# A hybrid decoder layer on one core: the first two F tiles by Strassen's products, interleaved

## The reference

```python
n = rmsnorm(h, ln1_g);  proj = n @ w_in                       # 1024 -> 1536 columns
y_pool = pool_mixer(...);  y_lru = rg_lru(...) * gelu(u_gate) # the two mixers, 512 wide each
mix = concat(rmsnorm(y_pool), rmsnorm(y_lru));  h = h + mix @ w_out
n2 = rmsnorm(h, ln2_g)
h = h + (silu(n2 @ w_ffn_gate) * (n2 @ w_ffn_up)) @ w_ffn_down   # D_FF = 2816 = 22 tiles of 128
return rmsnorm(h, lnf_g)
```

## Time and profile before

| | us |
|---|---|
| median of 3 runs (lowest, highest) | 896.62 (896.47, 896.67) |
| the profiled execution | 896.3 |
| its span, first to last instruction | 894.5 |
| PE busy | 882.7 (99%) |
| PEld busy | 725.7 (81%) |
| DVE busy | 613.7 (69%) |
| ACT busy | 396.1 (44%) |
| POOL busy | 273.6 (31%) |

### The profile page before, as it was taken

How to read it: one execution, slowest core, us unless ns; L and a number is a source line. 1 busy time by engine, 2 the same in 40 slices (tenths; PEclk the granted TensorE clock), 3 DMA queues, 4 the chain that set the end, 5 groups by cost and what they waited for, 6 DMA issues and landing times.

```text
span 894.5 us, 11037 instructions
## 1 busy us (share of the span) xinstructions
PE 882.7 (99%) x3980; PEld 725.7 (81%) x3980; DVE 613.7 (69%) x848; ACT 396.1 (44%) x654; POOL 273.6 (31%) x209
## 2 busy tenths in 40 slices
PE   7999999999999999999999999999999999999997
PEld 6877788888888888888888888888888888888886
DVE  5778996655679856556565664656638975787667
ACT  6689733533565323332233332333234444454456
POOL 0000032733345655545554555555540000000000
PEclk9999999999999999999999999999999999999999
DMA  9033011132020423223232332413239933333324
GB/s 322 9 96 93 24 48 48 47 118 71 1 72 0 150 75 130 83 95 136 88 130 74 102 130 69 156 56 121 95 107 377 398 104 96 95 96 99 101 83 188
DMA packets 94318, 98.01 MB, mean 110 GB/s; under 512 B 5764, under 2 KB 63672, under 8 KB 94264
## 3 DMA queue, kind: packets, MB, share of 16 engines
q1 hardware_dynamic: 83736, 78.16, 26.1%
q10 hardware_dynamic: 10528, 19.15, 7.1%
HBM read 70.81 MB, written 24.38 MB: 106 GB/s over the span
## 4 chain that ended last, share of the span: by engine, by line
PE 98%; DVE 1%; DMA 0%; ACT 0%; issue 0%; DVEq 0%; ACTq 0%
PE bank L2112 23%; PE bank L2113 23%; PE bank L2114 23%; PE bank L2000 5%; PE bank L2002 5%; PE bank L2001 5%; PE bank L1944 3%; PE bank L1945 3%; PE bank L1946 3%; PE bank L2021 1%; PE bank L1978 1%; PE bank L1957 1%; DMA h<-in_x 0%; PE bank L1966 0%; DVE nT_lo L1308 0%
## 5 line engine op out<-in xcount | busy, mean ns | idle before, releaser
L723 POOL TENSOR_TENSOR r_lo<-gu_raw,r_hi 128x512 fp32r<-128x512 f32 x84 | 115.7, 1378 | 83.4 <-ACT r_hi L1023 83.3
L723 POOL TENSOR_TENSOR r_lo<-wsum_S,r_hi 128x512 fp32r<-128x512 f32 x63 | 98.1, 1558 | 109.6 <-ACT r_hi L1023 109.6
L2112 PE MATMUL bank<-T_hi,r_lo 128*128 128x512 f32 x336 | 130.8, 389 | 0.0
L2114 PE MATMUL bank<-T_hi,r_hi 128*128 128x512 f32 x336 | 130.7, 389 | 0.0
L2113 PE MATMUL bank<-T_lo,r_hi 128*128 128x512 f32 x336 | 130.7, 389 | 0.0
L2113 PE MATMUL bank<-d_lo,h_hi 128*128 128x512 f32 (+1 forms) x312 | 120.5, 386 | 0.0
L2114 PE MATMUL bank<-d_hi,h_hi 128*128 128x512 f32 (+1 forms) x312 | 120.5, 386 | 0.0
L2112 PE MATMUL bank<-d_hi,h_lo 128*128 128x512 f32 (+1 forms) x312 | 120.5, 386 | 0.0
L1023 ACT CAST r_hi<-gu_raw 128x512 fp32r<-128x512 f32 x84 | 52.2, 621 | 143.6 <-PE bank L2114 143.6
L2112 PE MATMUL bank<-nT_hi,r_lo 128*128 128x512 f32 x252 | 98.0, 389 | 0.0
L2113 PE MATMUL bank<-nT_lo,r_hi 128*128 128x512 f32 x252 | 98.0, 389 | 0.0
(11 more groups left out here) (247 smaller groups left out, 1637.5 us busy)
## 6 DMA issues: line engine op xcount, KB each, us to landing
h_raw<-hid_ops ACTq DMA_DIRECT2D x72, 256.0 KB, 2.6
gu_raw<-in_w_ffn_gate SPq DMA_DIRECT2D x22, 512.0 KB, 3.7
gu_raw<-in_w_ffn_up SPq DMA_DIRECT2D x22, 512.0 KB, 4.8
hid_ops<-hid SPq DMA_DIRECT2D x44, 256.0 KB, 2.3
dn<-in_w_ffn_down SPq DMA_DIRECT2D x44, 256.0 KB, 9.8
hid_ops<-hsum_S SPq DMA_DIRECT2D x33, 256.0 KB, 2.6
w_raw<-in_w_in SPq DMA_DIRECT2D x11, 512.0 KB, 4.5
h<-in_x SPq DMA_DIRECT2D x8, 512.0 KB, 6.6
```

The lines of the kernel that those rows point to most:

```text
L723: pool.tensor_tensor(lo_of(n)[:], a_block(f, name), f32(hi_of(n)[:]), ALU.subtract)\
L2112: pe.matmul(bank, s_lo, m_hi, start=(opens and j == 0), stop=False, skip_group_check=True)
L2114: ins = pe.matmul(bank, s_hi, m_hi, start=False, stop=(closes and j == n - 1), skip_group_check=True)
```

## The change

- **F tiles 0 and 1 both by Strassen's products, interleaved.** The order is M1, M2, M3, M6, M7, M5, M4 and each product is done for f = 0 and then for f = 1. 15 products become 14. M3 gets a PSUM bank of its own in these two tiles, and `gate_second` adds two banks there. The last two token tiles are turned after the first and after the second product. Entries are numbered anew: the first four are A11 and A12 of both tiles, entries 4 and 5 S4, 6 and 7 S2, 8 and 9 S3, 10 and 11 S1, 12 and 13 A22.
- **Preparation.** The weight sums of F tiles 0 and 1 are made during the token tiles m = 3 to 6 of stage 2. T1's sum is apart (`t1_sum`), its first part ahead of the last variance of stage 2. `nT_hi` and `nT_lo` of B12 aren't made any more (B12 enters only through the T sums); GpSimd makes the low parts of B22 (`nT_lo_c`), VectorE those of B21 (`nT_lo_b`).
- **Operations.** VectorE's sums of two SBUF tensors there (weight sums, T sums, low parts of T and of B21, the last step of the reciprocal root) are scalar_tensor_tensor with a scalar of 1.0 instead of tensor_tensor.
- **Loads.** F tile 1's up weights no longer wait for the end of stage 2; F tile 2's weights wait for entry 12, F tile 3's for entry 13.
- **The beginning of stage 1.** In `project` the high times high and low weights come first, the low activations last; for (c, i) = (1, 0) all passes with the weights' low part come at the end. ScalarE takes the last squares of the first four tiles after two of the second half's casts.
- `sq_scr` and the low part of the last w_out piece move to other places; the latter is written in three instructions instead of two.

```diff
-        SECOND = ("M1", "M2", "M6", "M7", "M5", "M4", "M3")
+        FIRST = ("M1", "M2", "M3", "M6", "M7", "M5", "M4")
         def entry(f, pr):
-            return 4 + 7 * (f - 1) + products(f).index(pr)
+            return 2 * FIRST.index(pr) + f if f < 2 else 7 * f + PRODUCTS.index(pr)
...
         def chain_bank(f, c):
-            return psum[(4 if f == 1 else 3 * (f % 2)) + c]
+            return psum[(4, 2, 6)[c] + f] if f < 2 else psum[3 * (f % 2) + c]
...
             for f in range(2, FT):
-                sp_q.wait_ge(r_lo_ok, 4 if f == 2 else entry(f - 2, "M3") + 1)
+                sp_q.wait_ge(r_lo_ok, entry(f - 2, "M4" if f < 4 else "M3") + 1)
                 load_gu(f)
...
+            def combine(out_, a, b, op):
+                return dve.scalar_tensor_tensor(out=out_, in0=a, scalar=1.0, in1=b, op0=ALU.mult, op1=op)
...
+            def t1_sum(g):
+                s1, s2 = t_part(g, 0), t_part(g, 1)
+                dve.wait_ge(raw_ok, 2 * (5 + 2 * g) + 1)
+                dve.wait_ge(nlo_a_ok, 2 * g + 2)
+                combine(raw[0][:, :, s1], raw[0][:, :, s2], raw[0][:, :, s1], ALU.subtract).then_inc(t_ok, 1)
+
             def t_sums(g):
                 s1, s2 = t_part(g, 0), t_part(g, 1)
...
                 dve.wait_ge(t_ok, 3 * g + 1)
-                dve.tensor_tensor(raw[0][:, :, s2], raw[1][:, :, s2], raw[0][:, :, s2], ALU.subtract).then_inc(t_ok, 1)
-                dve.tensor_tensor(raw[1][:, :, s2], raw[1][:, :, s2], raw[0][:, :, s1], ALU.subtract).then_inc(t_ok, 1)
+                dve.wait_ge(raw_ok, 2 * (5 + 2 * g) + 2)
+                combine(raw[0][:, :, s2], raw[1][:, :, s2], raw[0][:, :, s2], ALU.subtract).then_inc(t_ok, 1)
+                dve.wait_ge(nlo_c_ok, 2 * g + 2)
+                combine(raw[1][:, :, s2], raw[1][:, :, s2], raw[0][:, :, s1], ALU.subtract).then_inc(t_ok, 1)
...
+            t1_sum(1)
             t_sums(1)
-            hidden1(0)
             t4_sums()
-            weight_sums(1, ("S1",))
-            for name, g in T_HI[0:4]:
+            for name, g in T_HI[0:5]:
                 t_lo(name, g)
-            hidden2(0)
-            for name, g in T_HI[4:6]:
+            second_sum(0)
+            t_lo("T1", 1)
+            second_sum(1)
+            for name, g in T_HI[6:]:
                 t_lo(name, g)
+            third_sum(0)
+            third_sum(1)
+            up_second(0)
+            gate_second(0)
+            weight_sums(2, ("S1",))
+            up_second(1)
+            gate_second(1)
+            hidden2(0)
+            up_first(0)
+            hidden1(0)
+            weight_sums(2, ("S4",))
+            up_first(1)
+            hidden1(1)
+            hidden2(1)
...
+                if (c, i) == (1, 0):
+                    pe.wait_ge(w_hi_ok, w_count(1))
...
+                if late:
+                    pe.wait_ge(w_lo_ok, w_count(1))
+                    for k in range(KT):
+                        ins = pe.matmul(bank, lo_[:, k], nT_hi[:, k, half(0)], start=False, stop=(k == KT - 1))
...
+            gate_up_product(0, "M1")
+            transposes(2 * TT - 2, xs2)
+            gate_up_product(1, "M1")
+            transposes(2 * TT - 1, xs2)
+            for pr in FIRST[1:]:
+                for f in range(2):
+                    gate_up_product(f, pr)
```

More of the change, by code:

```diff
@@ L357, in wo_low @@
         def wo_low(q, k):
-            return wo_lo3[k // 2][:, k % 2] if q == 3 else wo_lo[q % 2][:, k]
+            if q == 3:
+                return wo_lo3[:, k] if k < 2 else wo_lo3_end[k - 2][:]
+            return wo_lo[q % 2][:, k]
         t2 = t2b[:]
@@ L1065, in silu1 @@
                 p = f // 2
[L1066 to L1071, removed]
+                act.wait_ge(ent_ok, done(entry(f, "M2")))
+                if f == 1:
+                    act.wait_ge(r_lo_ok, entry(1, "M3") + 1)
                 if p > 0 and f % 2 == 0:
@@ L1157, in split_dn @@
                 act.copy(d_hi[s % STEPS][:], dn[D_BLOCK[pr], k][:]).then_inc(d_hi_ok, 1)
-            for f in range(1, FT):
-                for pr in products(f):
+            for f in range(2, FT):
+                for pr in PRODUCTS:
                     n = entry(f, pr)
-                    if pr == "M1" and f >= 2:
+                    if pr == "M1":
                         copy_m1(f)
@@ L1280, in rsqrt @@
                 if ready is None:
-                    step(dve.tensor_tensor(out_, out_, tmp_, ALU.mult))
+                    step(combine(out_, out_, tmp_, ALU.mult))
                 else:
@@ L1637, in t_lo @@
                 dve.wait_ge(t_hi_ok, T_HI.index((name, g)) + 1)
-                dve.tensor_tensor(T_lo[b][:, :, c], raw[b][:, :, c], f32(tile[:, :, t_part(g, j)]), ALU.subtract)\
+                combine(T_lo[b][:, :, c], raw[b][:, :, c], f32(tile[:, :, t_part(g, j)]), ALU.subtract)\
                     .then_inc(t_lo_ok, 1)
@@ L1766, in _ @@
+            up_first(0)
[4 more added lines that the diff above has]
+            hidden2(1)
+            for f in range(2, FT):
+                second_sum(f)
+                if f == 2:
+                    hidden_sums(0)
+                if f + 1 < FT:
+                    weight_sums(f + 1, ("S1",))
+                third_sum(f)
+                up_second(f)
                 if f + 1 < FT:
@@ L1993, in project @@
                 _, hi_, lo_ = w_tiles(c)
+                bank = pj[u % 4][:]
+                late = (c, i) == (1, 0)
                 for n, k in enumerate(X_ORDER[i]):
```

408 lines of the change are left out of this document (206 added, 202 removed).

## The result

The kernel after takes **900.47 us** (median of six, 898.96 to 900.82) against 896.64 for the kernel before (896.44 to 896.91): ratio 1.004, 95% interval 1.0028 to 1.0052. It is slower by 3.8 us where 2.2 were forecast, and the 900.8 at the upper end of the stated range just holds it. The profiled execution has a span of 899.0, 4.5 more than before, and is the longest of its six.

A forecast was written before the change was run, and what follows sets the result against it. PE, busy 882.7 of 894.5 us, was taken as the bound. Terms -2.7 - 0.5 + 3.4 + 0.3 + 1.2 + 0.5 = +2.2 gave 898.8 us (chance 0.38; own range 897.6 to 900.2, stated range 892.8 to 900.8).

The forecast's parts named there:

- Rival 1: VectorE and GpSimd overlap ahead of M6 of F tile 0, so no wait there: 893.4 us, chance 0.30.
- rival 3: F tile 2's weights land 1 to 2 us later than 295.3 and delay its first product: 900.2 us, chance 0.10.
- The product: F tile 0 takes seven products instead of eight, saving PE 12 matmuls, 2.72 us.
- Stage 1: PE's gaps near 14 and 17 us close at the beginning of stage 1: 0.5 us saved, bounds 0.2 and 0.6.
- rival 4: The product is saved but stage 1's 0.5 us isn't, as the DMA feeds it; inside all ranges, no separate chance.
- M6: F tile 0's seventh product waits 3.4 us for T sums, as VectorE and GpSimd exclude each other; bounds 2.9 and 4.0.
- u3: The hidden sums of F tiles 0 and 1 follow in one heap and put off u3: 0.5 us.
- After it, 0.3: Following M6, M7 of F tile 0 waits for u2, behind the low part of T1: 0.3 us (0 to 2).
- the upper bound there: If GpSimd waits for several VectorE instructions in a row, entry 7 is late by 3 x 1.2, costing another 2 us.
- Costs that something hides: Stage 2's added weight sums, 2.0 us in token tiles 3 and 5, are covered by VectorE's idle 1.8; 0.2 left over.
- u2 of F tile 2: Entry 12 delays F tile 2's load, VectorE stands before its weight sums, PE waits for u2: 1.2 us.
- Rival 2: VectorE catches up: M6 waits 3.4 us and nothing else does, 896.8 us, no change; chance 0.22.

The follow-up runs named there:

- engine: The kernel after, with four of GpSimd's subtractions ahead of M6 made by VectorE instead: 898.90 us, ratio to before 1.0025.
- twice: The kernel after, with GpSimd making each of four subtractions ahead of M6 twice, with the same result: 905.27 us, ratio to before 1.0095.
- tt: The kernel after, with its sums by tensor_tensor instead of scalar_tensor_tensor with a factor of 1: 899.92 us, ratio to before 1.0037.
- stage1: The kernel before, with only the change's part in stage 1: 896.06 us against 896.59, ratio 0.9995.
- Early: The kernel after, with F tiles 0 and 1's weight sums in token tiles 0 to 2 of stage 2 instead of 3 to 6: 899.05 us, ratio to before 1.0025.
- Order: The kernel after, with VectorE's first weight sum of F tile 2 moved behind three sums that need no load: 899.55 us, ratio to before 1.0032.
- combo2: combo, with F tile 2's first weight sum one place earlier and its u3 ahead of F tile 3's weight sums: 894.93 us, ratio to before 0.998.
- combo: The kernel after with the edits of engine, Order and Early at once: 896.81 us, ratio to before 1.0003.

## Why the prediction was right or wrong

**Where it held.** The direction, and the mechanism that makes it: VectorE and GpSimd take turns. Moving GpSimd's four instructions away (engine) and doubling them (twice) moved the stalls up to M6 by -1.7 and +5.0 with VectorE's list growing in the one and unchanged in the other. Rival 1, which wanted side by side, is refuted by both. The form of the sums changes nothing (tt). The size is another matter: 900.47 lies above the forecast's own range (897.6 to 900.2), and the figure nearest to it is that of rival 3, whose mechanism no trace shows.

**The terms.** The product: 2.72, as forecast. Stage 1: 0.5 forecast, 0.5 by the median of stage1, 0.6 by the traces; rival 4 fell. M6: 3.4 forecast, 2.94 measured. From the end of the last `normalise` to M6 I had 15.4; it took 14.86 (262.21 to 277.07), and the 0.54 between them are the nine 0.06 added for the longer form, which isn't longer: two such sums take 2.36 at 272.30, a step of 1.14 as before. The 1.28 that I had taken it from is that of `normalise`, which multiplies by a column and a row. u3: 0.5 and 0.47. "After it, 0.3" stood for u2 of F tile 0; the stall came at the next product instead, 0.52, and from entry 7. Its cause is ScalarE's queue, which the prediction lists: GpSimd stood 7.04 for the cast and then needed 2.12 (278.23), one turn; it did not wait for several of VectorE's, as the upper bound there had it.

**The step that failed** is "Costs that something hides". I set the weight sums of stage 2 against VectorE's idle 1.8 us in a token tile and found 0.2 left over. But the sums fall where GpSimd splits the first four entries. The same exclusion that I used for M6 makes one of the three sums 1.77 instead of 0.68, and it does so again in later token tiles. Nor does the running ahead of PE cover it: what is late is not a bank but `normalise`. The last one ended at 262.21, where I had 261.0, so PE waited 0.96 for xs where I had written "no stall". Early took the sums out of these token tiles; that `normalise` ended at 260.64, and the stall was gone. That the meetings with GpSimd decide, and not the sums' own length, is an estimate from rows: the two that take 1.77 and 1.78 add 2.2 us, more than the 1.2 by which `normalise` is late.

**The term mis-sized** is u2 of F tile 2: 1.2 forecast, 1.96 measured. The chain was the one I named (entry 12, the load, VectorE before its weight sums). VectorE got its load at 295.84 instead of 295.3, and behind it four of its instructions, not three, met one of GpSimd at 1.73 to 1.78 each, and a fifth took 1.00. Order shows that the wait hung in the main on the standing before the load: with other work there, u2 comes 2.5 earlier, 0.8 of it by an earlier load. Rival 3 (the load holds up the first product) had no stall in any trace of the kernel after. Rival 2 would have had M6 alone.

0.96 + 0.76 + 0.2 (entry 7) + 0.4 (small steps) - 0.46 (M6) - 0.1 (stage 1) = 1.8: from 2.2 to 3.95.

## What to carry to other kernels

If two engines take turns at a resource, apply it to every stretch in which both have work, the ones written down as "hidden" too; a helper's instruction then costs its time twice, once on its own engine and once on the other. An in-order list should wait for a load only behind all that needs no load. And a saved product is worth its matmuls only if everything that it wants earlier can be had earlier: here, with five places in the lists put right, 1.0 of the 2.72 us is left in combo2's trace (1.6 less, 0.6 of it from stage 1); the rest went into two waits and small steps.

## What the runs showed of the hardware

- **TensorE can fall to half its clock behind a stall.** In tt, behind the wait of 2.80, PE's timeline steps by 0.43 instead of 0.23, from 277.63 to 279.76:

```profile
277.07 0.77 PE L2184 MATMUL bank<-T_hi,r_lo 128*128 128x512 f32 x1 [2.80 <-DVE T_lo L1294]
277.63 0.63 PE L2185 MATMUL bank<-T_lo,r_hi 128*128 128x512 f32 x1
278.06 0.63 PE L2186 MATMUL bank<-T_hi,r_hi 128*128 128x512 f32 x1
```

  By stretches (us, then busy time of PE, PEld, DVE, ACT and POOL, granted clock, DMA) twice has 0.52 behind its stall of 4.8, near the lower level of 1.2 GHz, and full clock 6 us later:

```profile
282.00:288.00 6.00, 5.97 (x15) 4.69 (x16) 5.92 (x4) 0.41 (x1) 3.24 (x2) 0.52 0.00 0
288.00:294.00 6.00, 6.00 (x28) 4.96 (x27) 3.92 (x5) 3.35 (x5) 3.57 (x3) 1.00 0.00 0
```

  It came behind waits of 1.9, 2.4, 2.8, 2.8 and 4.8 us, and did not behind waits of 1.8, 2.1, 2.8 and 2.8 in the two traces of the kernel after, nor behind any of 1.3 or less. (The expectation of twice counts engine, whose half pace stands behind 1.9, among the waits of 2.4 or more.) Other runs of one kernel seem to differ in it too: of the six of the kernel after three have a mean granted clock of 0.996 or 0.997, where the profiled runs with half pace have 0.995 to 0.997, and three 0.999, as the one profiled. What tells these apart stays open.
- **The kernel after scatters.** The 21 runs of before beside twice, stage1 and combo keep within 1.1 us; the kernel after spreads over 1.9 in six, combo2 over 1.1 in eleven.
- **VectorE's sums of a PSUM bank and an SBUF tensor don't wait for GpSimd.** In the kernel after 15 of them lie inside a subtraction of GpSimd in stage 3, and none takes over 0.69, as at 308.87 above; sums of two SBUF tensors of that size take up to 1.80.
- **How the two engines share isn't fixed.** Besides the turns of one by one here, the kernel before has a row in which GpSimd waited for four of VectorE's; no trace of the kernel after or of tt repeats it.
